# Two-block transformer on one core: undivided query norm in the cross attention, the third chunk's inverse begun in the mixer projection, decays behind the rounding of weights

## The reference, cut to what matters

```python
x = x + _memory_cross_attention(_rms_norm(x, norm_cross_g[l]), _rms_norm(mem, norm_mem_g[l]),
                                w_mem_q[l], w_mem_kv[l], w_mem_o[l])
```

```python
decay = jnp.exp(jnp.where(tril, gc[..., :, None] - gc[..., None, :], -jnp.inf))
lower = jnp.where(strict, jnp.einsum("bhncd,bhnkd->bhnck", kb, k) * decay, 0.0)
sol = lax.linalg.triangular_solve(lower, rhs, left_side=True, lower=True, unit_diagonal=True)
...
v_new = u_n - jnp.einsum("bhck,bhkv->bhcv", w_n, state)
o_n = jnp.einsum("bhck,bhkv->bhcv", qg_n, state) + jnp.einsum("bhcs,bhsv->bhcv", a_n, v_new)
state = state * gl_n[..., None, None] + jnp.einsum("bhck,bhcv->bhkv", kg_n, v_new)
```

## Time and profile before

| | us |
|---|---|
| median of three runs | 2024.37 |
| the profiled execution | 2023.35 |
| its span | 2021.4 |
| TensorE busy | 1883.2 (93%) |
| VectorE busy | 1051.1 (52%) |
| ScalarE busy | 753.3 (37%) |
| POOL busy | 109.7 (5%) |

### The profile page before, as it was taken

The page is one execution under the profiler, slowest core; times in us unless marked ns, Lnnn a source line. Parts: engine busy times, 40 slices in busy tenths (PEclk is TensorE's granted clock), DMA queues, the critical chain, the costliest instruction groups (busy, mean ns, idle before and its releaser), DMA issues.

```text
span 2021.4 us, 27517 instructions
## 1 busy us (share of the span) xinstructions
PE 1883.2 (93%) x10978; PEld 1448.4 (72%) x10978; DVE 1051.1 (52%) x2006; ACT 753.3 (37%) x1596; POOL 109.7 (5%) x104
## 2 busy tenths in 40 slices
PE   6999888998998869999879999999999999999997
PEld 5665567776554447778777888888876688888886
DVE  6767656353211148775655444644567654444444
ACT  4445754441111146623443322322345542222222
POOL 0000000001222104010210000000000000000000
PEclk9999988998999889999999999999999999999998
DMA  5100213439999952222002233232321132323221
GB/s 188 47 10 25 95 45 110 141 131 393 410 409 408 400 202 64 69 67 73 2 2 88 89 100 94 87 112 89 99 74 43 32 105 94 104 93 95 95 93 42
DMA packets 72622, 248.60 MB, mean 123 GB/s; under 512 B 9218, under 2 KB 11522, under 8 KB 71600
## 3 DMA queue, kind: packets, MB, share of 16 engines
q1 hardware_dynamic: 67088, 235.65, 33.2%
q0 software_dynamic: 5408, 11.19, 1.6%
HBM read 242.62 MB, written 12.59 MB: 126 GB/s over the span
## 4 chain that ended last, share of the span: by engine, by line
PE 73%; DVE 7%; DMA 4%; ACT 3%; issue 1%; POOL 0%; SPq 0%; DVEq 0%; POOLq 0%; ACTq 0%
PE ps_pair L299 18%; PE ps_pair L300 17%; PE ps_pair L301 17%; PE ps_pair L2050 5%; DMA w_places<-w_experts 2%; PE ps_turn L2645 2%; PE ps_pair L892 1%; PE ps_out L2061 1%; PE ps_shared L2061 1%; DMA split_acts_as_f<-w_experts 1%; PE ps_out L923 1%; PE ps_pair L2637 1%; PE ps_turn L2147 1%; DMA g<-rows_h,g_as_int 1%; DVE w_low L242 1%
## 5 line engine op out<-in xcount | busy, mean ns | idle before, releaser
L299 PE MATMUL ps_pair<-split_acts,w_high 128*128 128x512 f32 (+1 forms) x1816 | 722.5, 398 | 24.3 <-DVE split_acts L626 11.5
L301 PE MATMUL ps_pair<-split_acts,w_low 128*128 128x512 f32 (+1 forms) x1816 | 705.9, 389 | 0.0
L300 PE MATMUL ps_pair<-split_acts,w_high 128*128 128x512 f32 (+1 forms) x1800 | 699.3, 388 | 0.0
L299 PEld LDWEIGHTS ps_pair<-split_acts,w_high 128*128 128x128 f32 x1816 | 344.2, 190 | 107.3 <-issue 26.5
L242 DVE TENSOR_TENSOR w_low<-w_raw,w_high 128x1024 fp32r<-128x1024 f32 (+4 forms) x249 | 281.4, 1131 | 261.6 <-ACT w_high L236 260.1
L301 PEld LDWEIGHTS ps_pair<-split_acts,w_low 128*128 128x128 f32 x1816 | 343.7, 189 | 71.8
L300 PEld LDWEIGHTS ps_pair<-split_acts,w_high 128*128 128x128 f32 x1800 | 342.0, 190 | 67.4 <-issue 1.9
L236 ACT ACTIVATE w_high<-w_raw 128x1024 fp32r<-128x1024 f32 (+4 forms) x249 | 242.6, 975 | 147.1 <-PE ps_pair L301 144.8
L372 DVE TENSOR_TENSOR x<-x,ps_pair 128x512 f32<-128x512 f32 x80 | 54.9, 686 | 141.6 <-PE ps_pair L301 141.6
L2270 DVE TENSOR_TENSOR g<-g,ps_pair 64x256 f32<-64x256 f32 x31 | 13.2, 425 | 176.9 <-ACT g L2216 176.9
L3241 ACT ACTIVATE split_acts<-h 128x512 fp32r<-128x512 f32 x44 | 27.9, 633 | 200.2 <-DVE h L3254 200.2
(11 more groups left out here) (560 smaller groups left out, 2372.0 us busy)
## 6 DMA issues: line engine op xcount, KB each, us to landing
w_raw<-w_gu SPq DMA_DIRECT2D x88, 512.0 KB, 3.5
split_acts_as_f<-w_experts SPq DMA_DIRECT2D x42, 1024.0 KB, 20.1
w_places<-w_experts SPq DMA_DIRECT2D x35, 1024.0 KB, 17.0
w_raw<-w_down SPq DMA_DIRECT2D x32, 448.0 KB, 3.2
w_raw<-w_gdnin SPq DMA_DIRECT2D x26, 512.0 KB, 3.6
w_raw<-w_out SPq DMA_DIRECT2D x24, 512.0 KB, 3.5
x<-w_experts SPq DMA_DIRECT2D x12, 1024.0 KB, 20.4
w_raw<-w_down SPq DMA_DIRECT2D x16, 512.0 KB, 3.5
```

The lines of the kernel that those rows point to most:

```text
L299: pe.matmul(out, wh[:, k, :], self.high(k), start=(n == 0), stop=False)
L300: pe.matmul(out, wh[:, k, :], self.low(k), start=False, stop=False)
L301: last = pe.matmul(out, wl[:, k, :], self.high(k), start=False, stop=(n == self.kt - 1))
```

## The change

**Norm.** The query norm becomes `Deferred`: behind each tile of `out` ScalarE adds L620 to its square and VectorE L626 to its addition; the block L500/L516/L469 goes. The sum stands beside memkv's tile 1, the spread and a copy to `R_TILE` beside tile 3, and memq is evacuated by VectorE (`scaled`) and not by ScalarE. The split query lies in other buffers, so expert loads 1 and 2 wait for memq's products and evacuation. On VectorE, end of out and begin of memkv; before (`x_49` is x, `h_56` the normed query):

The diff, cut (the buffer names `INT[c]` that became `DEC[c]` in `decay` and `products` are left out, and of the old list only its head and end stand here):

```diff
-        n_cross = Norm("cross", KT, S, x_tile, lambda k: vec("norm_cross", k), h_tile, hi, lo,
-                       lambda e: wait_stage_evac(e, "out"),
-                       wait_dst=lambda e: (wait_products(e, "out")), early=True)
+        hi_q = lambda k: AR[:, (6, 7, 16, 17, 20, 21, 22, 23)[k], :]
+        lo_q = lambda k: HR[:, k, :] if k < 4 else GR[:, (1, 2, 3, 14)[k - 4], :]
+        n_cross = Deferred("cross", lambda k: vec("norm_cross", k), hi_q, lo_q, lambda e, k: wait_evac(e, BASE["out"] + k))
...
-        n_mem.sq = n_mem.total = H[:, 0:4, :].rearrange("p k s -> p (k s)")
+        n_mem.sq = n_mem.total = G[:, 4:8, :].rearrange("p k s -> p (k s)")
...
         fl.append(Linear("out", out_hi, out_lo, lambda k: s_diff.ready(k) if k < 4 else n_mo.ready(k - 4),
-                         *add_and_square(n_cross), beside=in_steps(n_mem, 0, 2, 4)))
+                         n_cross.take_act, n_cross.take_dve, beside=in_steps(n_mem, 0, 2, 4)))
+        fl.append(n_cross.rest())
+
+        def cross_root_tile(act):
+            need(act, "norm_pe", ("cross", "spread"))
+            done(act.copy(R_TILE, ps_m[:, :]), "norm_act", ("cross", "R"))
+
+        cross_root = On(tensor=n_cross.tensor_sum, scalar=n_cross.norm.scalar_root, vector=n_cross.norm.vector_root)
+        cross_spread = On(tensor=n_cross.tensor_spread, scalar=cross_root_tile,
+                          vector=lambda dve: need(dve, "norm_act", ("cross", "R")))
         fl.append(Linear("memkv", lambda k: mh[:, k, :], lambda k: ml[:, k, :], n_mem.ready,
-                         taker(lambda j: mk[:, j, :]), beside=in_steps(n_cross, 0, 0, 1)))
-        fl.append(Linear("memq", hi, lo, n_cross.ready, taker(lambda j: g(4 + j))))
+                         taker(lambda j: mk[:, j, :]), beside={1: [cross_root], 3: [cross_spread]}))
+        fl.append(Linear("memq", hi_q, lo_q, n_cross.ready, None, scaled(lambda j: g(4 + j))))
...
-                first = {0: lambda: wait_products(sp, "memkv"), 2: lambda: need(sp, *n_cross.ready(KT - 1)),
-                         3: lambda: wait_products(sp, "memq"), 5: lambda: need(sp, *cross.last),
+                first = {0: lambda: wait_products(sp, "memkv"), 1: lambda: wait_products(sp, "memq"),
+                         2: lambda: wait_stage_evac(sp, "memq"), 5: lambda: need(sp, *cross.last),
...
+        DEC = [INT[0], INT[1], ST, INT[3]]
...
+        ADDED = {0: 1, 2: 2, 1: 3, 3: 4}
...
+        def second_moves():
+
+            def vector(dve):
+                dve.wait_ge(tile_done, GDNIN_DONE)
+                done(dve.memset(RR[2][BLK:P, :, 0:BLK], 0.0), "c_dve", ("zero", 2))
+
+            def gpsimd(pool):
+                pool.wait_ge(tile_done, GDNIN_DONE)
+                pool.tensor_tensor(INT[2], DEC[2], wide(ident), ALU.add).then_inc(diagonal_added, 1)
+            return On(vector=vector, gpsimd=gpsimd)
...
-        at_tile(1, mix0_roots, On(scalar=gates_scalar, vector=gates_vector))
+        at_tile(1, mix0_roots, On(scalar=gates_scalar, vector=gates_vector), On(vector=masks_vector))
...
-        at_tile(3, decay(0, state_banks, gate_read), att_mem0.weighed(0))
-        in_tile(4, decay(1, state_banks, lambda q: ("c_dve", ("e", 0, q))))
-        at_tile(4, att_mem0.turned_over(0), att_mem0.scored(1))
+        at_tile(3, att_mem0.weighed(0))
+        in_tile(4, decay(0, state_banks, gate_read))
+        at_tile(4, decay(1, state_banks, lambda q: ("c_dve", ("e", 0, q))), att_mem0.turned_over(0), att_mem0.scored(1))
...
-        at_tile(20, query_norm(3, ps_m, query_squared(2)))
+        u, r = step_u, step_r
+        at_tile(20, query_norm(3, ps_m, query_squared(2)), decay(2, ps_t, lambda q: ("c_dve", ("R", 0, LEVELS - 1, q))))
+        in_tile(21, products(2, lambda q: ("c_dve", ("e", 2, q))))
         at_tile(21, query_norm(4, ps_o, query_squared(3)))
-        at_tile(22, query_norm(5, ps_m, query_squared(4)), rows_in(0, "KG", ps_s, lambda q: att_mem0.last))
-        in_tile(23, rows_in(0, "VR", ps_s, lambda q: ("c_dve", ("KG", 0, q))))
-        at_tile(23, inner(0, ps_s, lambda q: ("c_dve", ("VR", 0, q))), On(vector=query_roots_vector))
+        in_tile(22, turned_root(2))
+        at_tile(22, query_norm(5, ps_m, query_squared(4)), u(2, 1), rows_in(0, "KG", ps_s, lambda q: att_mem0.last))
+        in_tile(23, r(2, 1), rows_in(0, "VR", ps_s, lambda q: ("c_dve", ("KG", 0, q))))
+        at_tile(23, u(2, 2), inner(0, ps_s, lambda q: ("c_dve", ("VR", 0, q))), On(vector=query_roots_vector))
+        in_tile(24, r(2, 2))
+        at_tile(24, u(2, 3))
+        in_tile(25, r(2, 3))
+        at_tile(25, u(2, 4))
...
-        steps = [On(tensor=gdnin_read), decay(2, ps_lin, lambda q: ("c_dve", ("kq", 0, q))),
-                 products(1, lambda q: ("c_dve", ("kq", 0, q))), products(2, lambda q: ("c_dve", ("R", 0, LEVELS - 1, q))),
...
-                  r(3, 4), read_state(3, lin_free(3)), feed_early(6, 8), u(3, 5), feed_early(0, 2), r(3, 5), feed_early(2, 4),
...
+        steps = [On(tensor=gdnin_read), second_moves(), products(1, lambda q: ("c_dve", ("kq", 0, q))), r(2, 4), solved(0),
+                 into(1, "KG", ("kq", 0)), u(2, 5), turned_root(1), into(1, "VR", ("KG", 1)), next_state(0), r(2, 5),
+                 gate_silu(0), gate_silu(1), u(1, 1), outputs(0, lambda q: ("c_dve", ("VR", 1, q))), join_u(2),
+                 gate_silu(2), gate_silu(3), r(1, 1), join_r(2), u(1, 2), gate_silu(4), gate_silu(5), normed(0), r(1, 2),
+                 gated(0), u(1, 3), decay(3, ps_lin, lin_read), r(1, 3), products(3, joined(2)), into(2, "KG", ("e", 3)),
...
+                 r(3, 5), from_state(3), normed(2), join_u(3), gated(2), join_r(3), read_state(3, lin_free(3)), solved(3),
+                 feed_early(6, 8), feed_early(0, 2), outputs(3, other_free(3)), feed_early(2, 4), feed_early(4, 6), normed(3),
+                 gated(3), feed_late(0), feed_late(1)]
```

68 lines of the change are left out of this document (26 added, 42 removed).

## The result

The changed kernel takes 2009.92 us, the median of five runs (2006.24 to 2013.14); the kernel before took 2023.97 in the same measurement (2020.46 to 2027.67, five runs). The ratio is 0.9943, with a 95% interval of 0.9927 to 0.9959: 11.5 us less, 8.3 to 14.8. The profiled execution took 2007.3 us, its span is 2005.3.

A forecast was written before the change was run, and what follows sets the result against it. TensorE, busy for 93% of the span, was taken as the bound, so its waits, clock and work count. 2023.35 - 11.0 + 3.3 - 2.1 = 2013.55, plus 1.0 to the median gives 2014.5 us; range 2004 to 2020.5.

The forecast's parts named there:

- cross norm: memkv to memq: VectorE's query block goes, so the stretch takes 24.7 us instead of 35.8; gain 11.0.
- the loss in B: Mixer tile 2 to the matmuls behind chunk 0's root: moved masks and decays were to lose 3.3 us.
- the gain in C: Chunk 0's root to out0's first matmul: the third chunk's earlier inverse was to gain 2.1 us.
- rival 3: memkv: late w_low cuts the norm's gain to 5 us, 2020.5 at worst; chance 0.06.
- The expert stage: Streamed experts: bound by transfers, yet the stream starts earlier and the norm's whole 11.0 us passes through.
- Rival 2: Streamed experts: the expert stream takes back the norm's gain, 2025.5 us, no change; chance 0.11.
- Decays: Mixer tiles 3 to 5: decay(0) waits about 1.2 us, TensorE idles 5 ahead of decay(1); loss 3.3.
- e0: VectorE's half of decay(0), which decay(1) waits for: its first half, 0.8 us, was to be there at 789.5.
- Third chunk, tiles 20 to 25: Mixer tiles 20 to 25: the third chunk's inverse adds 13.2 us of TensorE work, 0.8 of wait covered.
- The chain: Chunk chain: work falls to 76.6 us, waits to 8.1, plus 2.0 for the clock; 97.6 with the tail.
- The tail: Chain's end, x3's matmuls to out's first tile: 13.8 us instead of 7.1, as feeds delay the norm.
- rival 4: New chain: short waits among small matmuls keep the clock low, 2036 us with 25 us so; chance 0.04.

The follow-up runs named there:

- root_at_0: Changed kernel with the query norm's sum beside memkv tile 0 and the spread beside tile 1; 2015.60 us, one run.
- norm_alone: The kernel before with the norm's part of the change alone; 2010.43 us, ratio 0.9951 to the kernel before.
- decays_mixed: Changed kernel with decay(0) back beside mixer tile 3, decay(1) left beside tile 4; 2004.77 us, one run.
- feeds_early: Changed kernel with two out0 feeds ahead of read_state(3), one behind solved(3), one behind outputs(3); 2009.55 us, ratio 0.9943 to the kernel before.
- feeds_split: Changed kernel, decays as before, feeds early, last feed's ScalarE half ahead of chunk 3's squares, VectorE half behind outputs' addition; 2003.47 us, 0.9914 of the kernel before.

## Why the prediction was right

It said 2014.5 us, 9.9 less than before, with a range of 2004 to 2020.5; measured are 2009.92 and 11.5 less by the ratio. The cross norm, which makes up the gain, was right in mechanism and size; the loss in B was put 0.7 too low and the gain in C 1.9 too low, and that these two errors have opposite signs is luck. Step by step:

- **Cross norm.** Predicted 24.7 us from memkv to memq and a gain of 11.0; measured 24.80 and 11.0. The cover in the out projection held (rival 3 is out: no wait on L242), with less to spare than I had put it. The low parts of the weights for memkv tiles 2 and 3 are

```profile
328.53 2.36 DVE L242 TENSOR_TENSOR w_low<-w_raw,w_high 128x1024 fp32r<-128x1024 f32 x2
```

  so the first was there at about 329.7, some 0.3 us ahead of tile 2 at 330.03, where I had 1.4 ahead of memkv. The sum would have had to wait: root_at_0 finds it 2 us behind TensorE.
- **The expert stage.** I let the gain pass whole. norm_alone shows it, with 0.9951 and a stretch that moved and did not grow. Rival 2 is out.
- **Decays.** Predicted waits 1.2 and 5 and a loss of 3.3; measured 0.95 and 6.36 and 4.0 (B). The step that was too low is VectorE's queue beside POOL. The convolution ran in it from end to end and took 3.52 us, the price of tile 3, while my 788.7 (789.80 less 1.6) has only 0.5 of those 1.2 us more; the rounding took 1.85 us and not 1.53, L2544 0.83 and not 0.47. So `e0`'s first half was there at 776.7, 10.7 us behind decay(0)'s start, where I had 9.4. The rest came as priced: decay(1), the transposes and the scores took 6.3 us at partly low clock, for 4.0 + 2.2. My own terms add up to 789.5 + 6.2 = 795.7 and a loss of 2.8; the 796.2 and 3.3 that I wrote hold 0.5 that no term of mine gives, and hid a part of the error. decays_mixed undoes all of it.
- **Third chunk, tiles 20 to 25.** Predicted 13.2 - 0.8 = 12.4 more; measured 12.2.
- **The chain.** I named waits of 0.4, 0.7, 1.2, 2.2, 1.9, 0.3 and 1.4; the list has 0.6, 0.8, 1.4, 2.0, 2.1 and 1.3 in this order, and none for my 0.3. Both large waits of the earlier trace rows are gone.
- **The tail.** Right in kind, a little too dear: from the end of x3's matmuls (1038.2) 12.8 us against 13.8 predicted and 7.1 before. The term that was mis-sized is the second pair of feeds, which I had let follow one another on the two engines; VectorE began its two halves (1.83 us from 1045.12) under ScalarE's, and the root came at 1047.06. Over the whole chain TensorE is busy for 77.98 us, where I had 76.6 + 2.0 = 78.6, and idle for 17.8, where I had 19.0: that is why C gained 4.0 and not 2.1. feeds_early and feeds_split show that the feeds cause 4.2 of the 8.0 us of the wait.
- **The clock.** 0.94 over the chain as before; rival 4 did not come. But my sentence that by the trace only stretches behind a gap of 4 us or more are at risk was wrong: already in the kernel before, the first matmuls of `out` at 277.76 us run 0.77 and 0.63 us behind waits of 2.16 and 0.64, and in the new chain single waits of 2.0 and 2.1 us cost 1.4 us more in some executions (last section).

The sum was -11.0 + 3.3 - 2.1 = -9.8; the trace gives -11.0 + 4.0 - 4.0 = -11.0. Between the two profiled executions lie 16.05 us, so 5.0 more: 2.8 from the cross attention to the mixer projection and 2.3 behind `out0`. No edit touches the second; the first has the edits to memq's evacuation, the expert loads and the masks in it. The eleven other kernels with the new norm range there from 4.6 us less to 0.3 more than the kernel before, and behind `out0` from 2.2 less to 0.5 more. The ratio over all runs, 11.5 us (8.3 to 14.8), has room for at most 4 of them, so I take most of the 5 for the spread of executions; that none is of the change is not shown.

## What to carry to other kernels

Following each engine's written order with the durations of the old trace gave every new wait of a rewritten chain over 0.5 us to a few tenths of a microsecond; what was missed lay where two engines work on one step in turn, or beside a third. When a step is moved to fill another engine's gap, look at what it then stands behind on the engine that finishes it: decay(0)'s move saved 3.0 us of one wait and cost 6.4 in the next. And a filler (a feed, a copy) belongs ahead of the last dependent chain or, engine by engine, into its waits; a stage need not be moved as a whole.
